# Half of the expert gates by adding indirect DMAs into a cleared table, key lists searched in the query stage

## What is computed

```python
def one_block(xb):
    qry = jnp.einsum('td,de->te', xb, w_query).reshape(PEER_BLOCK, PEER_HEADS, 2, D_KEY // 2)
    s = jnp.einsum('thjd,jkd->thjk', qry, keys)           # 8 heads, 2 lists of 128 keys each
    s_top, i_top = lax.top_k(s, PEER_TOPK)                # 16 best of each list
    cand = s_top[:, :, 0, :, None] + s_top[:, :, 1, None, :]
    cand_idx = i_top[:, :, 0, :, None] * N_KEYS + i_top[:, :, 1, None, :]
    best, pos = lax.top_k(cand, PEER_TOPK)                # 16 experts of 16384 per head
    idx = jnp.take_along_axis(cand_idx, pos, axis=-1)
    gates = jax.nn.softmax(best, axis=-1)
    act = jax.nn.gelu(jnp.einsum('thkd,td->thk', peer_u[idx], xb), approximate=False)
    return jnp.einsum('thk,thkd->td', gates * act, peer_v[idx])
```

## Time and profile before

| | |
|---|---|
| median of 3 runs | 2417.23 us (2413.54 to 2417.33) |
| profiled execution, own time | 2415.77 us |
| its span | 2414.0 us |
| mean granted clock of TensorE | 0.973 |
| busy: PE, DVE, ACT, POOL | 2290.0, 1559.7, 895.1, 870.3 us |
| query stage | 721.8 to 828.8 us from the span's start |
| first to last hidden matmul | 850.5 to 1699 us |

### The profile page before, as it was taken

One profiled execution on the slowest core, in us unless ns is written; L12 is line 12 of the kernel. 1 busy time (PEld: TensorE's weight loads), 2 busy tenths in 40 slices (PEclk: granted clock), 3 DMA queues, 4 the chain that ended last, 5 costly groups with the idle time before them and its releaser, 6 DMA issues.

```text
span 2414.0 us, 34120 instructions
## 1 busy us (share of the span) xinstructions
PE 2290.0 (95%) x12943; PEld 1960.4 (81%) x12943; DVE 1559.7 (65%) x3465; ACT 895.1 (37%) x1179; POOL 870.3 (36%) x422
## 2 busy tenths in 40 slices
PE   5999999977989999999899999999999999999998
PEld 4998889755658988888788888888888888888886
DVE  4676569564633168887899997786565555555552
ACT  3434445551223233323245554455332222222221
POOL 0332336135523247657600210001554444444441
PEclk8999999977999999999999999999999999999998
DMA  7222122656656345555456997576564555545530
GB/s 273 68 81 66 58 69 74 169 159 185 196 201 154 90 123 140 136 152 144 118 140 182 276 266 206 155 224 201 220 259 176 189 209 191 190 177 207 198 150 35
DMA packets 307412, 392.73 MB, mean 163 GB/s; under 512 B 14545, under 2 KB 257637, under 8 KB 302914
## 3 DMA queue, kind: packets, MB, share of 16 engines
q1 hardware_dynamic: 212162, 302.86, 40.6%
q10 hardware_dynamic: 91664, 75.54, 9.6%
q0 software_dynamic: 3456, 12.58, 1.7%
HBM read 305.70 MB, written 81.26 MB: 160 GB/s over the span
## 4 chain that ended last, share of the span: by engine, by line
PE 60%; DVE 3%; POOL 2%; issue 0%; ACT 0%; DMA 0%; DVEq 0%; ACTq 0%; POOLq 0%
PE bank L2626 29%; PE bank L2081 25%; PE bank L2577 4%; POOL utL_hid L2064 2%; DVE work L2300 1%; DVE work L2301 1%; PE bank L2582 1%; PE bank L2567 1%; DVE utL_hid L2071 0%; DVE ut_hid L2051 0%; DVE work L2009 0%; DVE work L1993 0%; POOL work L1993 0%; DVE work L2455 0%; PE bank L2646 0%
## 5 line engine op out<-in xcount | busy, mean ns | idle before, releaser
L2081 PE MATMUL bank<-pH,utH_hid 128*128 128x512 f32 x1024 | 405.3, 396 | 4.4 <-POOL utL_hid L2064 4.4
L2081 PE MATMUL bank<-pH,utL_hid 128*128 128x512 f32 x1024 | 399.1, 390 | 0.0
L2081 PE MATMUL bank<-pL,utH_hid 128*128 128x512 f32 x1024 | 399.0, 390 | 0.0
L2626 PE MATMUL bank<-area,work 128*128 128x512 f32 x1536 | 350.8, 389 | 0.0
L2626 PEld LDWEIGHTS bank<-area,work 128*128 128x128 f32 x1536 | 288.3, 188 | 59.9
L2238 POOL TENSOR_TENSOR work<-work,work 128x1024 fp32r<-128x1024 f32 x64 | 155.5, 2432 | 368.5 <-ACT work L2485 368.5
L2064 POOL TENSOR_TENSOR utL_hid<-ut_hid,utH_hid 128x1024 fp32r<-128x1024 f32 x66 | 182.5, 2765 | 175.7 <-PE bank L2081 146.7
L864 PE MATMUL ps_in<-hH_in,wH_in 128*128 128x260 f32 x816 | 237.4, 291 | 2.4 <-DVE projarea L915 1.4
L2399 DVE TENSOR_TENSOR utL_hid<-u_hid,utH_hid 128x512 fp32r<-128x512 f32 x64 | 147.5, 2305 | 135.3 <-ACT utH_hid L2489 135.3
L864 PE MATMUL ps_in<-hL_in,wH_in 128*128 128x260 f32 x816 | 231.7, 284 | 0.0
L864 PE MATMUL ps_in<-hH_in,wL_in 128*128 128x260 f32 x816 | 231.4, 284 | 0.0
(11 more groups left out here) (535 smaller groups left out, 4458.0 us busy)
## 6 DMA issues: line engine op xcount, KB each, us to landing
u_hid<-in_peer_u_dram SPq DMA_DIRECT2D x256, 256.0 KB, 5.0
work<-in_peer_v_dram SPq DMA_DIRECT2D x64, 1024.0 KB, 4.8
hidden_dram<-ge_hid ACTq DMA_DIRECT2D x64, 512.0 KB, 2.6
gates_dram<-area ACTq DMA_DIRECT2D x16, 2048.0 KB, 11.9
wb_in<-in_w_in_dram SPq DMA_DIRECT2D x26, 1024.0 KB, 5.1
wstage<-in_w_ada_dram SPq DMA_DIRECT2D x32, 512.0 KB, 5.0
area<-hidden_dram SPq DMA_DIRECT2D x16, 1024.0 KB
area<-gates_dram SPq DMA_DIRECT2D x16, 1024.0 KB
```

The costliest lines, as they stand in the source:

```text
L2081: mm = self.nc.tensor.matmul(self.pa[u % 2][:, :], w[:, k, :], x[:, k, :], start=(n == 0), stop=(n == 3 * KD - 1))
L2626: mm = nc.tensor.matmul(bank[k], v[s][:, j, cols], w[s][:, j, :], start=(start and x == 0), stop=(stop and x == 2))
```

## The change

**Scores and lists.** The query stage now scores a chunk as soon as it is evicted: ACT copies a chunk to one of three small buffers, PE scores the four tiles of chunk n - 2 behind the products of chunk n, ACT copies the result, and DVE searches the list for all four tiles (13 lists; the last `LATE` = 3 in units 0 to 5 of the hidden stage). The first block of `peer_u` is loaded and transposed in the query stage.

**Scattered gates.** For the first two tiles (`SC` = 2) no one-hots are made. Candidate numbers are built as addresses of single numbers in a table in DRAM (token, row and column), gates are written with a token per partition, and POOL issues 2 x 128 indirect DMAs, each adding 128 gates (one per token) to the table. A head's 16 DMAs are issued together; the next head's wait until they have landed. SP clears the table with 32 stores of 512 KB at the end of the query stage. In the mixing stage half of a group's gates come from this table, half from the other.

**Selection.** Every subtraction is on DVE (`move_low`), POOL has none. `select` has eleven steps per tile, placed by `steps_by_unit` from unit 6 to 70; the picks of all heads are on DVE, two heads at a time. 64 quads are left, from unit 58 on.

```diff
+def steps_by_unit():
+    return {2 * LATE + 3 * n // 2: divmod(n, STEPS) for n in range(NC * STEPS)}
 def quads_by_unit():
     counts = [0] * UNITS
-    for u in range(62, 68):
+    for u in range(58, 74, 2):
         counts[u] = 1
...
+    rest = total - sum(counts)
+    for n in range(TAIL - 74):
+        counts[74 + n] = (n + 1) * rest // (TAIL - 74) - n * rest // (TAIL - 74)
...
@@ query stage, SP @@
+            sp.wait_ge(q["zeroed"], 1)
+            for g in range(NG):
+                sp.dma_start(scattered[g].rearrange("i (c b) e -> i c (b e)", c=ZPARTS),
+                             bcast(zero, 1, ZPARTS)).then_inc(q["zero_out"], 16)
...
+            sp.wait_ge(q["zero_out"], 16 * NG)
...
@@ query stage, ACT and PE @@
+                evict(n - 2)
+                if n >= 3:
+                    keep(n - 3)
...
+            def score(n):
...
+                for t in range(NC):
+                    mm = nc.tensor.matmul(quad[n % 2][:, t, :], qry[n % QR][:, t * L:(t + 1) * L], S.keysT[:, n % 2, :], start=True, stop=True)
+                mm.then_inc(q["scored"], 1)
...
+                if n >= 2:
+                    score(n - 2)
...
@@ query stage, DVE @@
-            for n in range(CHUNKS):
-                dve.wait_ge(q["product"], n + 1)
-                V.tensor_copy(halves(qry[:, n, :]), ps[n % 2][:, :, 0:HN]).then_inc(q["evicted"], 1)
+            V.memset(zero, 0.0).then_inc(q["zeroed"], 1)
+            for n in range(CHUNKS - LATE):
+                dve.wait_ge(q["kept"], n + 1)
+                best_of_list(V, own, S.lists[n], S.wk, S.top[:, :, n, :], S.idx[:, :, n, :], range(NC))
...
@@ expert stage, POOL @@
+            def scatter(i, h):
+                pool.wait_ge(located, PH // 2 * i + h // 2 + 1)
+                if h:
+                    pool.wait_ge(spread[i], 16 * TOPK * h)
+                for n in range(h * TOPK, (h + 1) * TOPK):
+                    pool.indirect_dma_start(out=cells, out_offset=bass.IndirectOffsetOnAxis(ap=address_of[i][:, n:n + 1], axis=0),
+                                            in_=gate_of[i][:, n:n + 1], in_offset=None, compute_op=ALU.add).then_inc(spread[i], 16)
+            for i in range(SC):
+                for h in range(PH):
+                    scatter(i, h)
             for u in range(UNITS):
-                if u + 1 < FIRST_DVE:
-                    H.move_low(pool, u + 1)
...
@@ expert stage, DVE @@
+            def locate(i, part):
+                if i < SC:
+                    at = slice(2 * TOPK * part, 2 * TOPK * (part + 1))
+                    V.tensor_copy(address_of[i][:, at], K.ei[:, at]).then_inc(located, 1)
...
+                elif s == 5:
+                    if i < SC:
+                        dve.wait_ge(m["gates"], i + 1)
+                        K.gates(own, gate_of[i])
+                    K.numbers(own, 0)
+                    locate(i, 0)
+                    own(K.find(1))
...
             for u in range(UNITS):
-                if FIRST_DVE <= u + 1 < UNITS:
-                    H.move_low_dve(dve, u + 1)
+                if u + 1 < UNITS:
+                    H.move_low(dve, u + 1)
...
+                if u + 3 < UNITS:
+                    H.turn(dve, u + 3)
+                if u < 2 * LATE:
+                    l = 2 * PH - LATE + u // 2
+                    best_of_list(V, own, S.lists[l], S.wk, S.top[:, :, l, :], S.idx[:, :, l, :], range(2 * (u % 2), 2 * (u % 2) + 2))
+                if u in STEP:
+                    select(*STEP[u])
```

More of the change, by code:

```diff
@@ L1730, with best_of_list, query_phase @@
 UNITS = NKEY
-def query_phase(nc, A, S, XH, XL, hT, qry, PH_, PL_, buffers, sample_rows, first):
+def best_of_list(V, own, src, wk, top, idx, tiles):
+    for half in range(2):
+        at = slice(8 * half, 8 * half + 8)
+        of = wk if half else src
+        for t in tiles:
+            last = V.max(top[:, t, at], of[:, t, :])
+        own(last)
+        for t in tiles:
+            last = V.max_index(idx[:, t, at], top[:, t, at], of[:, t, :])
+            if not half:
+                last = V.match_replace(wk[:, t, :], top[:, t, at], src[:, t, :], LOW)
+        own(last)
+def query_phase(nc, A, S, XH, XL, hT, PH_, PL_, buffers, sample_rows, first, scattered):
     per = 2
@@ L1738, in query_phase @@
     CHUNKS = 2 * PH
-    AHEAD = 5
     wv = A["peer_w_query"][0].rearrange("(k p) n -> p k n", p=P)
     BY_ACT = (1, 3, 5, 7)
+    AHEAD = 5
+    QR = 3
+    qry = [carve(S.work, AT_OH + N * i, (P, N)) for i in range(QR)]
+    keys = carve(S.work, AT_OH + N * QR + 8, (P, 2, P))
+    zero = carve(S.work, AT_QS + 384, (P, 512))
     with Phase(nc) as ctx:
-        sb = lambda n, s: ctx.enter_context(nc.sbuf_tensor(f"{n}_query", s, F32))
         sem = ctx.sem
@@ L1821, in _ @@
                     A_(halves(rows[:, :]), pt[0:B, :, :], ACT.Copy).then_inc(q["s_row"], 1)
+            for n in range(CHUNKS - 2, CHUNKS):
+                evict(n)
+                keep(n - 1)
+            keep(CHUNKS - 1)
         @block.tensor
@@ L1860, in _ @@
                     mm.then_inc(q["s_turned"], 1)
+                if n >= 2:
+                    score(n - 2)
+            score(CHUNKS - 2)
+            score(CHUNKS - 1)
         @block.vector
@@ L2459, in _ @@
         def _(act):
-            act.wait_ge(keys_t, 1)
-            nc.scalar.activation(keysT, quad[4][:, 0:2, :], ACT.Copy).then_inc(keys_s, 1)
+            H.move_high(act, 0)
+            H.move_high(act, 1)
             act.wait_ge(scored, 1)
             nc.scalar.activation(S.scS[:, :, :], quad[4][0:PH * B, 0:2, :], ACT.Copy).then_inc(kept, 1)
-            for n in range(16):
-                act.wait_ge(scored, n + 2)
-                nc.scalar.activation(S.sc[:, n // 4, 4 * (n % 4):4 * (n % 4) + 4, :], quad[n % 4], ACT.Copy).then_inc(kept, 1)
-                if n in (11, 13):
-                    H.move_high(act, (n - 11) // 2)
             def evict(q):
@@ L2551, in _ @@
             pe.sem_inc(mixed, 2 * JG)
-            pe.wait_ge(keys_in, 16)
-            nc.tensor.transpose(quad[4][:, 0, :], keys[:, 0, :], S.ident[:, :])
-            nc.tensor.transpose(quad[4][:, 1, :], keys[:, 1, :], S.ident[:, :]).then_inc(keys_t, 1)
-            pe.wait_ge(keys_s, 1)
-            pe.wait_ge(gathered, 1)
             for j in range(2):
@@ L2559, in _ @@
             mm.then_inc(scored, 1)
-            for t in range(NC):
-                for g in range(4):
-                    n = 4 * t + g
-                    if n >= 4:
-                        pe.wait_ge(kept, n - 2)
-                    for i in range(4):
-                        l = 4 * g + i
-                        mm = nc.tensor.matmul(quad[g][:, i, :], qry[:, l, t * L:(t + 1) * L], keysT[:, l % 2, :], start=True, stop=True)
-                    mm.then_inc(scored, 1)
             def place(q):
```

366 lines of the change are left out of this document (199 added, 167 removed).

## The result

The changed kernel takes **2521.46 us** (median of 4 runs, 2518.04 to 2522.47), against 2415.39 for the kernel before (4 runs, 2411.74 to 2417.33): the ratio is 1.0436, interval 1.0408 to 1.0463, so it is **slower by 4.4%**. The forecast was 2384.0, faster, with a range up to 2462.

A forecast was written before the change was run, and what follows sets the result against it. PE, busy 95% of the span, was taken as the bound. Hidden stage 849 - 56 (quads) + 7 (late scatter) = 800, with start +17, gave -32 from 2415.8: 2384 us, range 2350 to 2462 (forecast's own 2365 to 2400).

The forecast's parts named there:

- the period of a scatter DMA, c: POOL's scatter, hidden stage: one indirect DMA from start to start takes 1.4 us, between gather rows of 1.26 and 2.02.
- the meetings with VectorE: POOL in units 58 to 80: a subtraction every 6 us holds up about half its length, raising 1.26 to 1.4.
- The scatter's sum: POOL, hidden stage: 256 DMAs at 1.4 us plus 42 of landings make 400 us, 7 us late.
- landings: POOL between heads: each of 16 heads awaits a landing of 2.6 us before the next, 42 us together.
- The rule for hiding it: Hidden stage: a scatter of 393 us or less is hidden ahead of the samples' gathers; every us beyond is PE's.
- Begin and place: Scatter begins 79 us after the first hidden matmul; PE runs dry at the end of unit 83 if it is late.
- the prediction's sum: Whole kernel: hidden stage 849 - 56 + 7 = 800, start +17, so -32 from 2415.8: 2384 us.
- the start: Hidden stage's start: zeros landing at 861 move the first hidden matmul by 15 us, low clock adds 2: +17.
- Rival 1: POOL and DVE shut each other out: c = 1.62, scatter 457 us, kernel 2441, or 2543 at 2.02; chance 0.27.
- Rival 3: Adding stores of single numbers are slow in the DMA engines: scatter over 2000 us, kernel some 4000; chance 0.07.
- The quads: Hidden stage: 64 of 128 one-hot quads go, each 0.87 us of PE, -56 us, all on the path.
- The zeros: Query stage's end: 32 clearing stores behind a load at 804 take 55 us at 306 GB/s, landing at 861.

The follow-up runs named there:

- e5: Changed kernel with the 256 indirect DMAs writing their numbers without adding, so sums over heads are left out; 2368.36 us (one run).
- e7: Changed kernel with POOL awaiting the landing after every 8 scatter DMAs instead of every 16; 2567.03 us (one run).
- e9: Changed kernel with each of the 256 adding DMAs carrying the numbers of 64 partitions instead of 128; 2496.80 us (one run).
- e6: Changed kernel with the 256 indirect DMAs reversed, reading 128 single numbers each from the table without adding; 2384.53 us (one run).
- e10: Changed kernel with each of the 256 DMAs carrying 64 partitions' numbers instead of 128, and without the addition; 2373.90 us (one run).
- e8: Against the kernel with the scatter split around the samples' gathers: 12 of 32 zero stores issued early in the query stage; 2348.83 us, ratio 0.9729.

## Why the prediction was wrong

**The step that failed** is the period of a scatter DMA, c: "I take c = 1.4, nearer to the lower end". Both of its ends, 1.26 and 2.02, were rows of gathers, and the text said that an adding store of single numbers isn't in the trace. It measured 1.85 undisturbed. The step was wrong in its base, not in what it put on top: from 1.26 the prediction went to 1.40 for the meetings with VectorE, 0.14 x 256 = 36 us, and the meetings cost 26 us in the changed kernel and 38 in e5, which adds nothing and is otherwise the kernel that the prediction had priced. There c comes out as (401 - 34.4) / 256 = 1.43.

**The scatter's sum** in the changed kernel: from 942.94 to 1492.69, 549.8 us. 256 x 1.85 = 473.6, meetings 26, landings 40.2 (predicted 42, as 16 of 2.6; there are 14 of 2.9), and 10 of smaller waits. The addition alone is worth 256 x (1.85 - 1.26) = 151, which is the 150 above the predicted 400.

**The rule for hiding it** held: 393 us are hidden and every us beyond is PE's, so 549.8 - 393 = 157 was to be its wait, and PE waited 157.8. By the same rule e7's stretch (595.7) gives 203, e9's (523.4) 130, e6's (419.1) 26 and e5's (401.1) 8; PE waited 203.2, 132.7, 26.8 and 10.1. Only e10 is further off, 3 by the rule (395.5) and 11.4 in the trace. Begin and place held too: 79.4 us after the first hidden matmul (79), and the end of unit 83. With the measured length in the prediction's sum, 2384 + 150 = 2534, 12 above the profiled 2522.5. Of the 12, 4 are the start (+13.1, not +17), and the rest lies in the hidden stage, where 849 - 56 + 157 = 950 was 942.6: PE lost 8.5 of 50 us from 1200 to 1250 and now loses 3.6, where the prediction left that as it was.

**Rival 1** came near the time at its far end (2543 with every DMA at 2.02; its own sum, at c = 1.62, gave 2441), and for a wrong reason. The lock that it names is real, and 26 us of 550; with VectorE idle, where it can't act, the DMAs were as long as ever. It would have left e5 as slow as the change.

**Rival 3** named the right operation and the wrong place: the adding store was slow in POOL, which issues it, not in the DMA engines (its landings are the 2.9 us of e7, not 8.4).

**The quads**: 64 x 0.87 = 56 was right. PE is busy for 60.5 us less over the span, and the units without a quad stayed at 5.44, as two of ACT's GELUs, two units apart, show against the earlier trace rows:

```profile
1061.61 0.60 ACT L2175 ACTIVATE harea<-bank 128x512 f32<-128x512 f32 x1 [3.83 <-PE bank L2166]
...
1072.49 0.60 ACT L2175 ACTIVATE harea<-bank 128x512 f32<-128x512 f32 x1 [3.83 <-PE bank L2166]
```

**The zeros** landed when predicted (861; SP went on at 860.93), by two errors that cancelled. They were issued 7 us late (811.4, not 804). SP's fourth weight load left at 779.25, not at 771.38: the samples' row, which stands ahead of it, left 4.5 us later than before, and 4 of the 36 issues between the two are new (2 us). The row before and after:

```profile
748.84 0.48 SPq L1770 DMA_DIRECT2D sample_rows_dram<-rows_query  x1
```

```profile
753.31 0.30 SPq L1790 DMA_DIRECT2D sample_rows_dram<-work  x1
```

And the zeros took 50 us where 55 were predicted: the first window above shows 405 GB/s, not the 306 taken. The late load, for which PE waited 6.4 us, also put PE's end of the stage at 849, not at 844, which the zeros hid until e8 took them away.

## What to carry to other kernels

A DMA whose form isn't in the trace needs a price of its own. Where a queue of 256 hangs on it, measure one before the rest is costed, or give the forecast a case for a base price half as high again; the bounds of 1.26 and 2.02, from other forms, held the 1.85 only because of a lock that had no part in it. Before a long run of issues goes on a queue that also serves a later step, look for what stands behind it: here the same work split around the gathers was worth 161 us (2521.46 to 2360.55). And a store or load that hides under a wait shows its own lateness when the wait is removed, so look at the boundary again after each step.

## What the runs showed of the hardware that was not expected

- An indirect DMA of 128 single numbers holds POOL for 1.55 us when it adds to memory and 0.96 when it writes; reading 128 numbers takes 0.95, and reading 128 rows of 4 KB 0.95 to 0.98. Most of it is per DMA: at 64 numbers it is 1.41 and 0.89.
- A POOL DMA that begins inside a two-input operation of VectorE is longer by about what is left of that operation (43 of them, 0.60 us on average, against 0.72 left); one that is under way when the operation begins is not longer at all (63 of them).
- After the wait of 158 us at a granted clock of 0.50, PE had 0.53 from 1500 to 1510 and full speed from 1510 on, as these windows show: the pause cost little beyond itself.

```profile
1500.00:1510.00 10.00, 6.50 (x21) 5.50 (x22) 10.00 (x25) 2.10 (x2) 4.55 (x4) 0.53 0.54 181
1510.00:1520.00 10.00, 10.00 (x54) 8.55 (x53) 7.96 (x21) 3.16 (x4) 1.53 (x2) 1.00 1.02 271
```
